# Scan of a Mamba-2 layer: segment sums as differences of running sums, read by DMA, in place of matmuls

## What is computed

```python
a_cs = jnp.cumsum(a, axis=2)                      # a = dt*A, chunks of 128 tokens
seg = a_cs[:, :, :, None] - a_cs[:, :, None, :]
decay_ls = jnp.where(causal, jnp.exp(jnp.where(causal, seg, 0.0)), 0.0)
cb = jnp.einsum("bclgn,bcsgn->bclsg", cm, bm)
y_diag = jnp.einsum("bclsg,bclsgk,bcsgkp->bclgkp", cb, decay_ls, xdt)
...
y_off = jnp.einsum("bclgn,bcgkpn,bclgk->bclgkp", cm, prev, jnp.exp(a_cs))
return (y_diag + y_off).reshape(bsz, t, *y_diag.shape[3:])
```

## Time and profile before

| | us |
|---|---|
| median of 3 runs | 2637.5 |
| lowest and highest of the 3 | 2637.17, 2639.19 |
| profiled execution: first to last instruction (span) | 2635.4 |
| PE busy | 2555.2 (97%) |
| DVE busy | 1713.5 (65%) |
| ACT busy | 999.0 (38%) |
| POOL busy | 735.7 (28%) |

### The profile page before, as it was taken

The page is one execution under the profiler, slowest core; times in us unless marked ns, Lnnn a source line. Parts: engine busy times, 40 slices in busy tenths (PEclk is TensorE's granted clock), DMA queues, the critical chain, the costliest instruction groups (busy, mean ns, idle before and its releaser), DMA issues.

```text
span 2635.4 us, 45547 instructions
## 1 busy us (share of the span) xinstructions
PE 2555.2 (97%) x18328; PEld 1751.1 (66%) x18328; DVE 1713.5 (65%) x2242; ACT 999.0 (38%) x1795; POOL 735.7 (28%) x474
## 2 busy tenths in 40 slices
PE   8899999999999999999999998899999999999998
PEld 5566666666655657777766665676656677777665
DVE  6686777778677898777611276595279877773023
ACT  5433333343324334334311255596353343342121
POOL 1132535444242113222112111154411122221120
PEclk9999999999999999999999999998999999999999
DMA  3111101011130211121311101100121111113111
GB/s 121 41 33 40 34 33 41 33 33 41 33 130 33 97 48 49 48 64 48 125 56 45 48 33 57 41 2 9 41 97 48 62 41 58 62 35 135 50 55 65
DMA packets 44909, 142.33 MB, mean 54 GB/s; under 512 B 3552, under 2 KB 19040, under 8 KB 44512
## 3 DMA queue, kind: packets, MB, share of 16 engines
q1 hardware_dynamic: 44768, 140.35, 15.7%
HBM read 126.56 MB, written 12.71 MB: 53 GB/s over the span
## 4 chain that ended last, share of the span: by engine, by line
PE 74%; DVE 12%; ACT 5%; issue 4%; DVEq 2%; POOLq 1%; DMA 1%; POOL 1%; ACTq 1%
PE PS L2107 18%; PE PS L2108 18%; PE PS L2109 18%; PE PS L2517 4%; PE PS L2519 4%; PE PS L2518 4%; DVE TT L1554 3%; PE PS L2363 1%; ACT BIG L1396 1%; PE PS L2370 1%; DVE BIG L1875 1%; PE PS L2354 1%; PE PS L2393 1%; DVE TT L1550 1%; DVE wlo L1456 1%
## 5 line engine op out<-in xcount | busy, mean ns | idle before, releaser
L2107 PE MATMUL PS<-R,whi 128*128 128x384 f16 (+1 forms) x2400 | 750.6, 313 | 15.6 <-DVE wlo L1456 14.7
L2108 PE MATMUL PS<-R,whi 128*128 128x384 f16 (+1 forms) x2400 | 750.1, 313 | 0.0
L2109 PE MATMUL PS<-R,wlo 128*128 128x384 f16 (+1 forms) x2400 | 749.7, 312 | 0.0
L2107 PE MATMUL PS<-BIG,whi 128*128 128x384 f16 (+1 forms) x1452 | 452.4, 312 | 7.9 <-issue 4.5
L1456 DVE SCALAR_TENSOR_TENSOR wlo<-stage,whi 128x1024 f16<-128x1024 f32 (+1 forms) x150 | 207.8, 1388 | 386.2 <-ACT whi L805 385.0
L2108 PE MATMUL PS<-BIG,whi 128*128 128x384 f16 (+1 forms) x1452 | 452.4, 312 | 0.0
L2109 PE MATMUL PS<-BIG,wlo 128*128 128x384 f16 (+1 forms) x1452 | 452.2, 311 | 0.0
L2107 PEld LDWEIGHTS PS<-R,whi 128*128 128x128 f16 x2400 | 236.5, 99 | 146.0 <-issue 27.1
L2108 PEld LDWEIGHTS PS<-R,whi 128*128 128x128 f16 x2400 | 236.6, 99 | 125.2 <-issue 10.5
L2109 PEld LDWEIGHTS PS<-R,wlo 128*128 128x128 f16 x2400 | 236.6, 99 | 120.3 <-issue 1.5
L723 POOL TENSOR_TENSOR BIG<-TT,BIG 128x1040 f32 (+1 forms) x44 | 99.1, 2251 | 483.6 <-ACT BIG L1292 483.5
(11 more groups left out here) (274 smaller groups left out, 4482.3 us busy)
## 6 DMA issues: line engine op xcount, KB each, us to landing
stage<-wa SPq DMA_DIRECT2D x164, 512.0 KB, 3.5
stage<-wd SPq DMA_DIRECT2D x32, 704.0 KB, 4.1
h_keep<-hT SPq DMA_DIRECT2D x2, 4160.0 KB, 11.7
hT<-h SPq DMA_DIRECT2D x4, 1536.0 KB, 11.1
hT<-h_keep SPq DMA_DIRECT2D x4, 1536.0 KB, 8.9
out<-hT SPq DMA_DIRECT2D x4, 768.0 KB, 3.5
hT<-h SPq DMA_DIRECT2D x2, 1088.0 KB, 9.8
hT<-h_keep SPq DMA_DIRECT2D x2, 1088.0 KB, 13.5
```

Source lines behind the costliest of these rows:

```text
L2107: eng.matmul(acc, WH[slot][:, ws], x(0, k, b), start=first, stop=False)
L2108: eng.matmul(acc, WH[slot][:, ws], x(1, k, b), start=False, stop=False)
L2109: return eng.matmul(acc, WL[slot][:, ws], x(0, k, b), start=False, stop=last)
```

## The change

Sums over the tokens l and s are no longer formed by matmuls. While it forms the three sets of sums before the first slot, PE also forms the running sums transposed (3 more f32 matmuls of 128 columns, heads and chunks on 96 partitions); ACT copies them to `csT` (and keeps the running sums themselves as `cs`, instead of their exponentials), and SP writes them to a DRAM tensor `cs_rows`, one row of 128 tokens for each chunk and head. For each chunk SP then reads 8 rows back onto all 128 partitions (`sums_over_tokens`: 512 KB into `seg`), POOL subtracts the sum of its own token from them and takes the minimum with 0 (`segments`, on POOL now), and ACT takes the exponential from SBUF.

The state's part of y is computed with S as the stationary operand: 4 f32 matmuls of 128 columns whose output is already in the layout of y, so that `y_turn` goes. The factor exp(running sum) is now needed along the free dimension: SP reads the rows of the 8 heads, each onto 64 partitions (`sums_by_head`, two DMAs, 256 KB together, into `EC`), ACT takes the exponential (`decays_by_head`, 128x512), and DVE multiplies with it. The last addition of `chunk_skip` reads two operands in SBUF, before one in PSUM. With banks 4 and 5 free of `segments`, the waits of PE for `ga_read` and `gb_read` ahead of `chunk_main` go; `root_a` on ACT waits for `ga_read` instead. On DVE the clamp and the split of dt*A go.

```diff
@@ -157,7 +157,7 @@
-        lower16 = sb("lower16", [P, P], F16)
+        EC = sb("EC", [P, HG * HD])
@@ -199,6 +199,7 @@
         hTh = hT[:, :, :].bitcast(F16).rearrange("p a b -> p (a b)")
+        cs_rows = nc.dram_tensor("cs_rows", (NCH * NH, P), F32, kind="Internal").ap()
         h_keep = nc.dram_tensor("h_keep", (P, KD, L), F32, kind="Internal").ap()
@@ -259,7 +260,7 @@
-        aU = [T2.bitcast(F16)[:, HG * P * i:HG * P * (i + 1)] for i in range(2)]
+        seg = T2
@@ -287,11 +288,11 @@
         xdt, xdtd, S, Y = aux(512), aux(512), aux(512), aux(512)
-        yD = Y
         brow, cbm = aux(P), aux(P)
         NE = NCH * NH
-        dtr, ar2, ecs, cdec, dd = aux(NE), aux(NE), aux(NE), aux(NE), aux(NE)
-        ar_p = [ar2.bitcast(F16)[:, NE * i:NE * (i + 1)] for i in range(2)]
+        dtr, cs, cdec, dd = aux(NE), aux(NE), aux(NE), aux(NE)
+        CSW = NE // 3
+        csT = BIG[0:CSW, 4, 0:3 * P]
         ar = BIG[:, 7, 0:NE]
@@ -504,6 +506,30 @@
+            def sums_over_tokens(n):
+                g, c = divmod(n, NCH)
+                T = CHUNK[c][1]
+                if n == 0:
+                    eng.wait_ge(dt_c, 4)
+                    eng.dma_start(cs_rows.rearrange("(i r) l -> r i l", r=CSW),
+                                  csT.rearrange("p (i l) -> p i l", i=3)).then_inc(cs_out, 16)
+                    eng.wait_ge(cs_out, 16)
+                else:
+                    eng.wait_ge(decay_ready, n)
+                rows = bass.AP(tensor=cs_rows.tensor, offset=(c * NH + g * HG) * P, ap=[[0, T], [P, HG], [1, T]])
+                eng.dma_start(seg[0:T, 0:HG * T].rearrange("p (h l) -> p h l", h=HG), rows).then_inc(cs_in, 16)
+            def sums_by_head(g, c):
+                if g * (NCH - 1) + c > 1:
+                    eng.wait_ge(y_scaled, g * (NCH - 1) + c - 1)
+                for o in range(2):
+                    rows = bass.AP(tensor=cs_rows.tensor, offset=(c * NH + g * HG + o) * P,
+                                   ap=[[0, HD], [2 * P, XT], [1, P]])
+                    eng.dma_start(EC[HD * o:HD * (o + 1), :].rearrange("p (j l) -> p j l", j=XT),
+                                  rows).then_inc(ec_in, 16)
             load_h(0)
@@ -513,6 +539,12 @@
                 load_unit(u)
+                g, s_ = divmod(u - 3 - GT, SLOTS)
+                if 0 <= g < NG and 1 <= s_ < NCH:
+                    sums_by_head(g, s_)
+                g, s_ = divmod(u - 2 - GT, SLOTS)
+                if 0 <= g < NG and s_ < NCH:
+                    sums_over_tokens(g * NCH + s_)
                 if u == U_OUT + KD + 3:
@@ -597,18 +627,17 @@
-            def decay_products(n):
+            def segments(n):
...
                 T = CHUNK[c][1]
-                if n > 0:
-                    eng.wait_ge(seg_sums, n)
-                for part in range(2):
-                    r = eng.tensor_tensor(aU[part][0:T, 0:HG * T].rearrange("p (h l) -> p h l", h=HG),
-                                          ar_p[part][0:T, ds(g * HG + c * NH, HG)].unsqueeze(2)
-                                          .broadcast_to([T, HG, T]),
-                                          upper[0:T, 0:T].unsqueeze(1).broadcast_to([T, HG, T]), ALU.mult)
-                r.then_inc(aU_ready, 1)
+                eng.wait_ge(cs_in, 16 * (n + 1))
+                t = seg[0:T, 0:HG * T]
+                th = t.rearrange("p (h l) -> p h l", h=HG)
+                eng.tensor_tensor(th, th, cs[0:T, ds(g * HG + c * NH, HG)].unsqueeze(2).broadcast_to([T, HG, T]),
+                                  ALU.subtract)
+                eng.drain()
+                eng.tensor_scalar(t, t, 0.0, None, ALU.min).then_inc(seg_ready, 1)
@@ -639,9 +668,8 @@
                 lows(0, b)
-            eng.wait_ge(dt_b, 1)
-            decay_products(0)
             eng.wait_ge(dt_c, 4)
+            segments(0)
             for g in range(NG):
@@ -656,7 +684,7 @@
                     if s < NCH and g * NCH + s + 1 < NG * NCH:
-                        decay_products(g * NCH + s + 1)
+                        segments(g * NCH + s + 1)
             gate_last(2)
@@ -932,9 +960,14 @@
                     eng.wait_ge(y_inside, n)
-                eng.wait_ge(seg_sums, n + 1)
-                eng.activation(Em[0:T, 0:HG * T].rearrange("p (a l) -> p a l", a=2),
-                               PS[0:T, 4:6, 0:HG * T // 2], ACT.Exp).then_inc(decay_ready, 1)
+                eng.wait_ge(seg_ready, n + 1)
+                eng.activation(Em[0:T, 0:HG * T], seg[0:T, 0:HG * T], ACT.Exp).then_inc(decay_ready, 1)
+            def decays_by_head(g, c):
+                m = g * (NCH - 1) + c
+                eng.wait_ge(ec_in, 32 * m)
+                eng.activation(EC[:, :], EC[:, :], ACT.Exp).then_inc(ec_ready, 1)
@@ -955,6 +988,7 @@
                 eng.preload_act_table_set("natural_log_exp_and_others")
+                eng.wait_ge(ga_read, 3)
                 eng.activation(sq_a, sq_a, ACT.Ln)
@@ -1103,9 +1137,10 @@
                 for n_ in {GT - 2: (0, 1), GT - 1: (2,)}.get(i, ()):
-                    dst, bank, scale = ((ecs, 6, 1.0), (dd, 7, 1.0), (cdec, 6, float(D)))[n_]
+                    dst, bank, scale = ((cs, 6, 1.0), (dd, 7, 1.0), (cdec, 6, float(D)))[n_]
                     eng.wait_ge(dt_acc, 2 + n_)
-                    eng.activation(dst, PS[:, bank, 0:NE], ACT.Exp, scale=scale).then_inc(dt_c, 1)
+                    eng.activation(dst, PS[:, bank, 0:NE], ACT.Copy if n_ == 0 else ACT.Exp, scale=scale)
+                    eng.activation(csT[:, n_ * P:(n_ + 1) * P], PS[0:CSW, bank, NE:NE + P], ACT.Copy).then_inc(dt_c, 1)
                 take(i, 0)
@@ -1133,6 +1168,8 @@
                     take(i, 1)
+                    if 1 <= s < NCH:
+                        decays_by_head(g, s)
                     if g > 0 and 2 <= s < 6:
@@ -1638,13 +1677,7 @@
             eng.drain()
-            eng.tensor_scalar(ar, ar, -60000.0, None, ALU.max)
-            eng.drain()
-            eng.tensor_copy(ar_p[0], ar)
-            eng.drain()
-            eng.tensor_tensor(ar_p[1], ar, ar_p[0], ALU.subtract)
-            eng.drain().then_inc(dt_b, 1)
+            eng.sem_inc(dt_b, 1)
@@ -1672,8 +1705,9 @@
                     eng.wait_ge(y_state, ns)
-                    eng.tensor_tensor(heads(Y, T), heads(PS[:, 2, :], T), per_head(g, c, ecs, T),
-                                      ALU.mult).then_inc(y_row_ready, 1)
+                    eng.wait_ge(ec_ready, ns)
+                    eng.wait_ge(y_d, g * NCH + c)
+                    eng.tensor_tensor(Y, PS[:, 2, :], EC[:, :], ALU.mult).then_inc(y_scaled, 1)
                 if c < NCH - 1:
@@ -1713,9 +1747,8 @@
                     eng.drain()
-                    eng.wait_ge(y_transposed, g * (NCH - 1) + c)
                     x_ = xc4(g)[:, :, t0:t0 + T]
-                    r = eng.tensor_tensor(x_, x_, PS[:, 2, :].rearrange("p (j l) -> p j l", j=XT)[:, :, 0:T], ALU.add)
+                    r = eng.tensor_tensor(x_, x_, Y.rearrange("p (j l) -> p j l", j=XT), ALU.add)
                 r.then_inc(y_d, 1)
@@ -2343,15 +2376,21 @@
                         eng.wait_ge(dt_c, 2)
-                    eng.matmul(PS[:, bank, 0:NE], m[:, :], ar, start=True, stop=True).then_inc(dt_acc, 1)
+                    eng.matmul(PS[:, bank, 0:NE], m[:, :], ar, start=True, stop=True)
+                    eng.matmul(PS[0:CSW, bank, NE:NE + P], ar[:, n_ * CSW:(n_ + 1) * CSW], upper[:, :], start=True,
+                               stop=True).then_inc(dt_acc, 1)
                 for b in range(3):
...
                 eng.wait_ge(state_new, g * (NCH - 1) + c)
-                eng.wait_ge(y_d, g * NCH + c)
-                eng.matmul(PS[0:T, 2, :], xc(g, 1)[:, t0:t0 + T], S, start=True, stop=True).then_inc(y_state, 1)
+                if g * (NCH - 1) + c > 1:
+                    eng.wait_ge(y_scaled, g * (NCH - 1) + c - 1)
+                for j in range(XT):
+                    r = eng.matmul(PS[:, 2, j * P:j * P + T], S[:, j * P:(j + 1) * P], xc(g, 1)[:, t0:t0 + T],
+                                   start=True, stop=True)
+                r.then_inc(y_state, 1)
@@ -2381,19 +2420,6 @@
-            def segments(g, c):
-                n, T = g * NCH + c, CHUNK[c][1]
-                if n > 0:
-                    eng.wait_ge(decay_ready, n)
-                eng.wait_ge(aU_ready, n + 1)
-                for a in range(2):
-                    w = HG * T // 2
-                    for p_ in range(2):
-                        r = eng.matmul(PS[0:T, 4 + a, 0:w], lower16[0:T, 0:T],
-                                       aU[p_][0:T, a * w:(a + 1) * w], start=(p_ == 0), stop=(p_ == 1))
-                r.then_inc(seg_sums, 1)
             def c_b(g, c):
@@ -2406,13 +2432,6 @@
-            def y_turn(g, c):
-                T = CHUNK[c][1]
-                eng.wait_ge(y_row_ready, g * (NCH - 1) + c)
-                for j in range(XT):
```

(18 more changed lines are left out.)

9 lines of the change are left out of this document (4 added, 5 removed).

## The result

The changed kernel takes 2614.5 us (median of 4 runs, 2613.0 to 2616.8) beside 2638.4 us for the kernel before on the same chip (4 runs, 2637.2 to 2639.7): ratio 0.9912, 95% interval 0.9901 to 0.9924. It is 23.8 us faster where 47.5 were forecast, and 2614.5 lies above the range of 2579 to 2610.

The account below looks back on a forecast made before the run. PE was taken to bound the kernel, busy for all of 100 us of the scan. 51.5 us come off, 4 are given back on DVE, 0 for the state's part: 2637.5 - 47.5 = 2590 us, range 2579 to 2610.

Parts of the forecast that it names:

- TensorE's terms: Work taken off PE in the scan comes off the time in full; a slot goes from 15.58 to 14.27 us.
- `y_turn` and the state's part: In each chunk's y: dropping the transposes saves 14.1 us; four f32 matmuls for the state cost 0 more.
- the waits at the means: PE's waits ahead of `chunk_main` at the group means, with the lower clock there, all go: 7.4 us.
- rival 2: The f32 weight loads in the state's part of y do not hide: 26 us more, 2616 us; chance 0.10.
- the circle: Loop of exponential, SP's read (4.5 us), POOL, next exponential: 9.6 us, hidden in a 14.27 us slot.
- rival 3: The read of the sums sets the slot; if it takes 12 us, 91 us more, 2681 us; chance 0.05.
- Rival 4: PE's waits at the group means only move elsewhere: 7.4 us back, 2597 us; chance 0.05.
- the gross sum: Everything coming off PE, plus DVE's saving before the first slot, before anything is given back: 51.5 us.
- the term of 4 us: DVE's last addition in "c" slots stands behind POOL's subtraction, 0.33 us late in 15 slots: 4 us given back.
- the paragraph on DVE and POOL: Weighs DVE and POOL as PE's nearest rivals in "c" slots: 1.56 us to spare ahead of `y_in_chunk`, 4 us lost.
- Rival 1: DVE becomes the bound: POOL's operations cost it 3.0 us per "c" slot; 18 us instead of 4, 2604; chance 0.20.
- The minimum's size: POOL's minimum with 0 on the sums, having one operand less, takes at most the subtraction's 1.89 us.

Follow-up runs that it names:

- y_only: The kernel before with only the state's part of y changed, reads by head as four DMAs, sums still by matmul: 2624.3 us, ratio 0.9951.
- mean_waits: The change with TensorE's three waits ahead of `chunk_main` at the group means put back: 2622.4 us, ratio 0.9946.
- on_act: The change with subtraction and minimum of the sums moved from GpSimd to ScalarE, as eight activations a chunk: 2584.4 us, ratio 0.9803.
- act_clamp: The change with only the minimum moved from GpSimd to ScalarE (Relu, then Exp); GpSimd still subtracts: 2598.6 us, ratio 0.9852.
- cheap_pair: The change with GpSimd's minimum replaced by a (mult, add) pair by 0.001 and 0: 2610.1 us, ratio 0.9896.
- idle_min: on_act plus two GpSimd minima over 128x512 of unused buffer as each read of sums lands, results unused: 2600.1 us.
- idle_pair: on_act plus two GpSimd (mult, add) operations over 128x512 of unused buffer as each read of sums lands, results unused: 2595.3 us.
- experiment 9: on_act plus two GpSimd operations nobody waits for per read; three kernels with (mult, add), subtraction or minimum: 2595.3, 2602.2, 2600.1 us.
- no_square: The change with GpSimd's seven sums of squares cut to one column, the minimum kept: 2604.2 us, ratio 0.9872.
- seg_only: The kernel before with only the running sums by DMA and GpSimd; the state's part of y and its transposes stay: 2616.1 us, ratio 0.992.

## Why the prediction was right and where it failed

**Right.** TensorE's terms: undisturbed slots of 14.32 us against 14.27; `y_turn` and the state's part at 13.4 us against 14.1 (`y_only`); the waits at the means at 7.9 against 7.4 (`mean_waits`). The four f32 matmuls take 0.98 us: rival 2 does not happen. The Trainium skill (TensorE: Matmul & The Clock Gate, Weight-path perf modes), whose rule that fast weight load does not apply to fp32 was weighed there, would have spoken for 26 us more; the trace shows none of them. The read lands after 4.9 us and the circle hides (rival 3). Rival 4 does not happen. The mask product (line 1737) is back at 1.23 us, as forecast, since GpSimd's mask products are gone.

`on_act` tests the gross sum, since it takes from GpSimd all that the change gave it. The forecast's median of 2637.5 less 51.5 is 2586.0; `on_act` gives 2584.4.

**Wrong: the term of 4 us.** The failing step is the paragraph on DVE and POOL, where the change gives back 4 us of "0.33 x 15 = 5". The change gives back 30.1 us (2614.5 - 2584.4): 16 with the minimum (`act_clamp`), 14.1 more with the subtraction (`on_act`). Three things in that step were off:
- *Which operation is hit.* It looked at the last addition, which mostly isn't hit (median 693 ns over 32, longest 1496). GpSimd starts as the read lands. In a "c" slot that is close to the turn of the slot (370.10 where the next slot starts at 371.96) and not the 4.6 us ahead of it that "near 474" means. So it and the sums of squares and decays queued behind it lie on the next three taps and the split, all with two SBUF inputs. Rival 1 names "its next taps", and its 3.0 us of VectorE per slot are near the 2.9 seen.
- *Which deadline counts.* It compared with `y_in_chunk`, with 1.56 us to spare, and so did rival 1. The nearer deadline is `c_b`, which waits for the addition to the state, with 1.0 us to spare in `on_act` and 0.4 in a slot with a sum of squares. The trace of before could have told it (below): 471.62 - (469.09 + 0.68) = 1.85 us, of which the change takes 0.87, since the four matmuls of `segments` stood ahead of `c_b` in the slot.
- *What a wait costs.* It counted a wait once. Three waits of 3.0 to 3.9 us in the changed kernel come with a stretch of 6.8 us at half clock each, some 3 us more per wait. The waits at `c_b` beyond those of `on_act`, 20.0 us, and these three stretches, some 9 us, make up nearly all of the 30.1 us; that is an estimate from the profiled executions.

Timelines of VectorE and TensorE, kernel before, the slot of the earlier trace rows (`y_in_chunk` at 463.04): the addition to the state and `c_b`:
```profile
469.09 0.68 DVE L1683 TENSOR_TENSOR AUX<-AUX,PS 128x512 f32<-128x512 f32 x1
...
471.62 0.38 PE L2404 MATMUL PS<-BIG 128*128 128x128 f32 x2
```

The minimum's size, "at most the same" as 1.89 us, was a miss as well: 2.77 alone and up to 3.8. With that size put right by `cheap_pair` the time is 2610.1, so this explains 4.4 of the 24.5 us by which the forecast was too low. The rest is rival 1's mechanism, whose 2604 was too mild for the two last reasons; it had been given a chance of 0.20. The bound on it (the minimum has one operand less, so it can't be dearer) was a guess in place of a row: the trace of before has no single-immediate `tensor_scalar` of this size. Its only one of about this size on GpSimd (line 667, 128x1040, two immediates) takes 1.16 us.

The rule of the Trainium skill (SBUF — State Buffer, Who interferes with whom), that a DVE instruction with two SBUF inputs and a reading GpSimd instruction exclude each other, agrees with the runs for GpSimd's `tensor_tensor`: the taps (two SBUF inputs) grow from 4.68 us to 6.78, 7.02 and 7.48 under GpSimd's work of three different kinds, while `idle_min`'s line 1731, with one input in PSUM, takes its 0.68 at 337.10 in the middle of a sum of squares. The prediction applied it to one addition and not to the taps and the split.

**Why length does not set the price.** Single taps tell it, one instruction each. A tap takes 1.30 us alone. One that starts while a `tensor_tensor` of GpSimd is under way ends 1.09 to 1.11 us after that operation's end, in 317 of 320 such taps of all traces. Single taps of VectorE and the sum of squares of GpSimd that each one met, in `on_act`, in the change and in `idle_pair`, then a tap beside a minimum in the change:
```profile
313.76 1.92 DVE L1612 SCALAR_TENSOR_TENSOR TT<-UB,pr,TT 128x1040 f32<-128x1040 f32 x1 [1.44 <-ACT TT L941]
312.12 2.46 POOL L659 TENSOR_TENSOR hT<-hT,BIG 128x1040 f32<-128x1040 f32 x1 [10.47 <-ACT BIG L979]
...
327.30 3.27 DVE L1603 SCALAR_TENSOR_TENSOR TT<-UB,pr,TT 128x1040 f32<-128x1040 f32 x1
...
317.53 3.08 DVE L1624 SCALAR_TENSOR_TENSOR TT<-UB,pr,TT 128x1040 f32<-128x1040 f32 x1 [2.59 <-ACT TT L953]
317.11 2.39 POOL L669 TENSOR_TENSOR hT<-hT,BIG 128x1040 f32<-128x1040 f32 x1
...
135.52 1.92 DVE L1603 SCALAR_TENSOR_TENSOR TT<-UB,pr,TT 128x1040 f32<-128x1040 f32 x1
134.50 3.57 POOL L640 TENSOR_SCALAR TT<-TT 128x1024 f32<-128x1024 f32 x1 [0.16 <-issue]
```
In `on_act` the sum of squares is nearly over when the first tap starts, and no tap takes more than 1.93 us. The added operations, however short, stand ahead of it in GpSimd's queue and push it onto the taps, and the one that meets it takes 3.08 us in `idle_pair`. In the three kernels of experiment 9 all 19 taps of over 2.5 us stand against a sum of squares or one of the gate's products (`gate`), none against an added operation. `no_square`, where the sums of squares are cut short, bears it out. That the pushing sets the price is read from these rows; no run moved the sum of squares alone. The minimum does not shut a tap out for its whole length: the tap of 135.52 to 137.44 lies inside a minimum of 134.50 to 138.07, and there the trace does not agree with a rule of whole instructions.

**What stays open.** How many us of the whole a given operation costs can't be worked out from this ahead of a run: an added GpSimd operation of 1.0 to 1.3 us a slot costs 9 to 12 us in all, one of 2 us 14 to 18, one of 2.8 us 14 to 16. An estimate that fits roughly: VectorE's work with two SBUF inputs in a "c" slot is 4.68 (taps) + 1.22 + 1.23 + 1.23 + 0.69 = 9.05 us, and with GpSimd's 1.90 + 2.77 + 2.82 + 2.04 = 9.53 (as they lasted in the late slot, waiting included) that is 18.6, more than the 14.32 of the slot; in `on_act`, with 2.4 + 2.04 left, it is 13.5 and fits. It says which slots are in danger, not by how much, and no run tested it by itself. Nor is it shown by a run why one wait of TensorE has a stretch at half clock and the next has none.

## What to carry to other kernels

Work moved to GpSimd is not free because GpSimd is idle: add its time to VectorE's two-input operations and compare the sum with the slot, then look at which of them it lands on, given when its input arrives, and onto which of them it pushes the GpSimd work that stands behind it. Measure slack at every step that waits for VectorE, not only at the last one, and price a wait of 3 us of TensorE at up to twice its length. Where ScalarE can form the same term (Relu with a bias and scale -1, then Exp with scale -1), it did so here beside VectorE at no measurable cost: the change with subtraction and minimum there takes 2584.4 us, 0.9803 of the kernel before.

## What the runs showed of the hardware

- GpSimd's `tensor_scalar` on 128x1024 float32: 2.77 us with one immediate, for min, max, mult and add alike; 1.04 us for (mult, add) with two (1.24 once); 3.63 us for (mult, min). The second immediate, an addition of 0, makes a multiplication 2.7 times as fast.
- Eight ScalarE activations of 128x128 with a bias per partition took 2.43 us, 0.30 each.
- A DMA that spreads 8 rows of 512 bytes of DRAM over each of 128 partitions, 512 KB in all, lands after 4.9 us (median of 32), where a weight load of the same size takes 3.5.
- A VectorE tap (128x1040, two SBUF inputs, 1.30 us alone) that starts within a GpSimd `tensor_tensor` ends 1.09 to 1.11 us after it (317 of 320); beside a GpSimd `tensor_scalar` with one immediate it can start and end inside it.
- TensorE's waits of 3.0 us and more in the scan of the changed kernel come with a stretch of 6.8 us at half clock each; in `seg_only` two waits of 3.1 us come with one of 3.4 us each. In `on_act` the clock was 1.00 through the whole stretch from 320 to 420 us, in which TensorE was busy throughout.
